# Memory projections as full-precision products of raw weights, a new division of the first convolution, and first-attention values with the value matrix stationary

## The chip, the cores and the metric

One Trainium2 chip; the kernel runs on one of its cores, as one launch. The time is the device time in microseconds (us) of that core. The kernel before takes 1420.38 us, the median of three runs (1419.74 to 1420.71). A core has five engines with a queue of instructions each: PE (TensorE, matrix products), DVE (VectorE), ACT (ScalarE), POOL (GpSimd) and SP (SyncE, which here only issues DMAs). Each executes its own queue in order; between engines only semaphores order the work.

## The reference, cut to what matters

Two transformer layers on 512 tokens of width 1024, all in float32. The change lies in the first:

```python
h = rmsnorm(x, norm_mix_g); proj = h @ w_in
q, k, v, qi, ki, wi, glu = split(proj)            # 8 query heads of 64, one key and value head
score = sum_h wi_h * relu(qi_h . ki)              # 4 index heads; keep the best 128 keys of a row
p = softmax(q . k / 8 over the chosen keys)       # 8 heads, 4 blocks of 128 queries
a_out = p @ v
u = causal_dwconv(ga * sigmoid(gg), conv_b_w, conv_b_b)   # 31 taps, 512 channels
b_out = silu(layernorm(u))                        # over the 512 channels
x = x + concat(a_out, b_out) @ w_out
hq = rmsnorm(x, norm_cross_g); m = rmsnorm(mem, norm_mem_g)   # mem: 256 rows of 1024
kc = m @ w_k_cross; vc = m @ w_v_cross            # the memory projections, two 1024 x 1024 weights
# then cross attention of hq on kc and vc, a feed-forward block, and the second layer
```

## The kernel before

Features lie on the 128 partitions and tokens on the free axis. Each weight matrix is streamed from HBM in chunks of 512 or 704 KB through two slots (`weights_raw`, slot = chunk number modulo 2). A chunk is split in two: ACT rounds it (`weights_high`, `high`, L661), POOL subtracts (`weights_low`, `low`, L584), and PE forms three products in the fast single-pass type for each block: high by high, high by low, low by high (`chunk`, L1615). The raw slot is free for the next DMA as soon as POOL has subtracted (`weight_low`).

The first layer up to the first part of its output projection is a plan written by hand, `FIRST_PLAN`: a list of items which every engine walks through in the same order, issuing its own part of each. After the 16 tiles of `w_in` come 35 steps. Step s holds, in this order: the logits of attention item s (PE L1820; an item is a head and a block of queries, 32 of them, in widths of 128, 256, 384 and 512 keys for 8 items each); on DVE the mask and row minimum (L1237); on ACT the exponential (L789); one to two "fills" taken from the list by `FILLS_AT`; the transposes of item s-2 (PE L1828, copied by ACT, L797); the values of item s-3 (PE L1839, p stationary, 64 columns of v moving); and taps of the convolution. A fill is half a chunk of a memory projection: 8 chunks for kc (256 columns, L1615), then 8 for vc (512 columns, L1725). ACT rounds chunk q+2 right behind chunk q (`fill_ends`).

The convolution has 4 blocks of 128 channels with 31 taps each. Two ways run side by side. `tap`: DVE multiplies and adds in one instruction (L1154), each waiting for the one before. `product`: ACT multiplies (L735) into one of two buffers, POOL adds (L633). ACT may start a product only when the addition two before it is done. Before, DVE has all taps of blocks 2 and 3 and the last 22 of block 1, in steps 0 to 24; ACT and POOL have block 0 and 9 taps of block 1, 40 products, 10 of which stand ahead of the steps and 30 in steps 0 to 23.

When all taps are there, step 25 has the mean of the layer norm (PE L1851, ones by conv), step 26 the variance (L1857), step 28 the spread of its factor over the partitions (`spread`, L1659) with four SiLU and four roundings on ACT (L814, L816), step 29 the low parts. From step 31 on, pieces of the output projection ("second", L1753) stand between the items. `norm` (DVE L1248) divides the values of a block of queries by their sums, `heads` (PE L1702) turns them, and `heads_out` splits them.

## Time and profile before

| | |
|---|---|
| median of 3 runs | 1420.38 us |
| the profiled execution: its time, its span | 1419.84 us, 1418.0 us |
| PE busy | 1367.1 us (96%) |
| DVE, ACT, POOL busy | 780.3, 539.2, 606.4 us |
| mean granted clock of PE | 0.983 of full |
| span of the 35 steps up to the first "second" piece | 131.1 to 253.2 us |

Times in rows are us from the start of the span unless marked ns. A matmul's row shows its whole passage through the array, so back-to-back rows overlap: the cost of one is read from start to start, not from its length. A float32 product shows as two records (x2), a product in the fast type as one, a float32 transpose as one.

### The profile page before, as it was taken

Reading aid. Unit: us, or ns where it says so; the run is one execution under the profiler, and the core shown is the slowest. Engines: PE = TensorE matmul, PEld = TensorE weight load, DVE = VectorE, ACT = ScalarE, POOL = GpSimd, SP = SyncE. Lnnn points to the kernel's source line nnn. Section 1 sums busy time; section 2 is a strip of 40 time slices with the busy share of each in tenths; the row PEclk is TensorE's granted clock in tenths of the full one; section 3 lists DMA queues with packets and bytes.
Section 4 is the critical chain, followed back from the end, with each engine's and each line's share of the span. In section 5 each row is a group of like instructions: output and inputs, shape, how many; then the busy total and the mean of one; then the engine's idle time right before and its main releaser. Section 6 shows DMA issues by size and latency. Waiting matters only on the chain.

```text
span 1418.0 us, 18066 instructions
## 1 busy us (share of the span) xinstructions
PE 1367.1 (96%) x6240; PEld 1096.9 (77%) x6240; DVE 780.3 (55%) x1091; ACT 539.2 (38%) x843; POOL 606.4 (43%) x295
## 2 busy tenths in 40 slices
PE   7999898999999999999999999999999999999997
PEld 5687776887777888888888777666778888888885
DVE  6698995253446777777523588655453333332222
ACT  4454667253333232223223353534342322323321
POOL 3487981342134444444444433122244444444341
PEclk8999999999999999999999999999999999999998
DMA  6122320121122232223322222111123232223321
GB/s 220 45 90 82 112 75 31 60 89 60 60 74 90 92 101 92 101 95 114 102 87 91 89 75 74 45 45 45 45 89 100 92 100 92 103 94 103 101 91 71
DMA packets 31876, 121.20 MB, mean 85 GB/s; under 512 B 3536, under 2 KB 3664, under 8 KB 31568
## 3 DMA queue, kind: packets, MB, share of 16 engines
q1 hardware_dynamic: 31392, 119.55, 25.0%
q10 hardware_dynamic: 432, 0.96, 0.3%
q8 instruction: 33, 0.54, 0.2%
q14 instruction: 19, 0.16, 0.0%
HBM read 118.40 MB, written 2.10 MB: 85 GB/s over the span
## 4 chain that ended last, share of the span: by engine, by line
PE 74%; issue 13%; POOL 5%; DVE 4%; ACT 2%; DMA 1%; POOLq 0%; SPq 0%; DVEq 0%; ACTq 0%
PE acc L1615 60%; POOL weights_low L584 3%; PE acc L1753 3%; POOL conv L633 2%; PE aux L1985 1%; PE aux L2005 1%; PE acc L1725 1%; PE aux L1987 1%; DVE aux L1154 1%; PE aux L1839 1%; PE aux L1820 1%; DVE a_low L1310 1%; DMA weights_raw<-w 1%; PE aux L1809 1%; PE aux L1995 1%
## 5 line engine op out<-in xcount | busy, mean ns | idle before, releaser
L584 POOL TENSOR_TENSOR weights_low<-weights_raw,weights_high 128x1024 fp32r<-128x1024 f32 (+1 forms) x204 | 524.6, 2572 | 781.9 <-ACT weights_high L661 778.9
L661 ACT CAST weights_high<-weights_raw 128x1024 fp32r<-128x1024 f32 (+1 forms) x202 | 221.8, 1098 | 511.3 <-PE acc L1615 478.8
L1615 PE MATMUL acc<-a_high,weights_high 128*128 128x512 f32 x976 | 390.0, 400 | 4.5 <-POOL weights_low L584 3.1
L1615 PE MATMUL acc<-a_high,weights_low 128*128 128x512 f32 x976 | 381.2, 391 | 0.0
L1615 PE MATMUL acc<-a_low,weights_high 128*128 128x512 f32 x976 | 380.8, 390 | 0.0
L1615 PEld LDWEIGHTS acc<-a_high,weights_high 128*128 128x128 f32 x976 | 183.9, 188 | 47.0 <-issue 6.3
L1615 PEld LDWEIGHTS acc<-a_low,weights_high 128*128 128x128 f32 x976 | 184.0, 189 | 39.5 <-issue 2.6
L1615 PEld LDWEIGHTS acc<-a_high,weights_low 128*128 128x128 f32 x976 | 183.8, 188 | 38.9
L1127 DVE TENSOR_TENSOR residual<-acc,residual 128x512 f32<-128x512 f32 (+1 forms) x64 | 44.0, 687 | 197.4 <-PE acc L1615 140.0
L1615 PE MATMUL acc<-h_high,weights_high 128*128 128x512 f32 x352 | 137.6, 391 | 0.0
L1615 PE MATMUL acc<-h_high,weights_low 128*128 128x512 f32 x352 | 137.0, 389 | 0.0
L1615 PE MATMUL acc<-h_low,weights_high 128*128 128x512 f32 x352 | 136.9, 389 | 0.0
L1392 DVE TENSOR_TENSOR h_low<-work,h_high 128x512 f32 x44 | 88.8, 2018 | 39.5 <-ACT h_high L892 39.5
L1386 DVE TENSOR_TENSOR work<-acc,row_factor 128x512 f32<-128x512 f32 x44 | 30.4, 692 | 105.5 <-PE acc L1615 105.5
L1615 PEld LDWEIGHTS acc<-h_high,weights_low 128*128 128x128 f32 x352 | 66.1, 188 | 13.8
L1615 PEld LDWEIGHTS acc<-h_high,weights_high 128*128 128x128 f32 x352 | 66.1, 188 | 13.5
L1615 PEld LDWEIGHTS acc<-h_low,weights_high 128*128 128x128 f32 x352 | 66.1, 188 | 13.4
L889 ACT ACTIVATE work<-work 128x512 f32<-128x512 f32 x44 | 27.8, 631 | 97.6 <-DVE work L1383 94.0
L1306 DVE TENSOR_TENSOR square_sum<-square_sum,square 128x512 f32<-128x512 f32 x20 | 51.5, 2576 | 20.2 <-ACT square L1040 9.9
L1154 DVE SCALAR_TENSOR_TENSOR aux<-glu,par,aux 128x512 f32<-128x512 f32 x78 | 58.8, 754 | 2.0
L1479 DVE TENSOR_TENSOR_SCAN left<-stay 128x128 f32<-128x128 f32 (+3 forms) x32 | 33.6, 1049 | 44.6 <-ACT stay L961 41.3
L1381 DVE SCALAR_TENSOR_TENSOR work<-gated,par,work 128x512 f32<-128x512 f32 x22 | 55.4, 2518 | 3.4 <-DVE work L1379 3.4
(347 smaller groups left out, 1920.2 us busy)
## 6 DMA issues: line engine op xcount, KB each, us to landing
weights_raw<-w SPq DMA_DIRECT2D x172, 512.0 KB, 3.2
weights_raw<-w SPq DMA_DIRECT2D x32, 704.0 KB, 4.0
residual<-xT SPq DMA_DIRECT2D x8, 256.0 KB, 7.2
out<-y_tok SPq DMA_DIRECT2D x4, 512.0 KB, 3.7
mem_raw<-memT SPq DMA_DIRECT2D x1, 1024.0 KB, 5.4
mem_tok<-mem SPq DMA_DIRECT2D x1, 1024.0 KB, 7.4
lru_weights<-blockdiag ACTq DMA_DIRECT2D x1, 512.0 KB, 3.4
sine<-positions ACTq DMA_DIRECT2D x1, 256.0 KB, 7.0
```

Source lines behind the costliest of these rows:

```text
L584: g.tensor_tensor(weights_low[:, s, 0:cols], weights_raw[:, s, 0:cols], weights_high[:, s, 0:cols].bitcast(F32), ALU.subtract).then_inc(we ...
L633: g.tensor_tensor(conv[:, b], conv[:, b], product[:, j % 2], ALU.add).then_inc(last_conv_steps, 1)
L661: a.copy(weights_high[:, s, 0:cols], weights_raw[:, s, 0:cols]).then_inc(weight_high, 1)
L1127: v.tensor_tensor(residual[:, bass.ds(n, 1)].rearrange("p a n -> p (a n)"), acc[:, s], residual[:, bass.ds(n, 1)].rearrange("p a n -> p (a ...
L1154: ins = v.scalar_tensor_tensor(dst, src, weight, sofar, ALU.mult, ALU.add)
L1306: v.tensor_tensor(total_ if to is None else to, total_, squares, ALU.add).then_inc(summed, 1)
L1381: own.then(v.scalar_tensor_tensor(work[:, 0], gated[:, 1:1 + T], dcol("fconv_w", c + 1), work[:, 0], ALU.mult, ALU.add))
L1386: v.tensor_tensor(work[:, 1], acc[:, 1], row_factor[:], ALU.mult).then_inc(tile_out[1], 1)
L1392: v.tensor_tensor(at(dst_low, i), work[:, 1], at(dst_high, i).bitcast(F32), ALU.subtract).then_inc(operand_low, 1)
L1479: own.then(v.tensor_tensor_scan(left[:, 0:w][:, ::-1], back, back, 1.0, ALU.mult, ALU.min))
L1615: last = t_.matmul(acc[:, bank, 0:cols], w[:, s, wide], x_[:, k0 + k, 0:cols], start=start and k == opens and n == 0, stop=stop and k == c ...
L1753: last = t_.matmul(acc[:, t], w[:, q % 2, wide], x_[:, block0 + k], start=k == 0 and n == 0, stop=k == 3 and n == 2)
```

## The change

- kc and vc are now float32 products straight from the raw chunk and from the scaled memory `m_raw`: one instruction for each block in place of three (L1731, L1742 of the new kernel). No rounding, no subtraction, no `m_high` and `m_low`. The gain of the memory norm is multiplied in by ACT, not POOL. A raw slot is now free only when PE has finished its chunk (`chunk_done`), for the 16 chunks of kc and vc and for the first two of the next matrix.
- The convolution: ACT and POOL take blocks 0 and 1 whole (62 products, 10 ahead of the steps and 52 in steps 0 to 21), DVE blocks 2 and 3 (62 taps in steps 0 to 20). Mean, variance, spread and low parts move from steps 25, 26, 28, 29 to 23, 24, 26, 27.
- Values: v is stationary, in two copies padded with zeros (`v_pad`), p moves with 128 columns, and the result comes out with features on partitions. The inverse sums are turned instead of the values: reciprocal (`total`) at step 8, 16, 24, 32, widened by ACT, turned by PE and copied by ACT one step later, multiplied in by DVE (`norm`) two steps later.
- `spread` turns the factor with a transpose in place of a float32 product, at all nine places where it is called.

```diff
-        m_high = sb("m_high", [P, KB, MB * P], F32R, s1)
-        m_low = sb("m_low", [P, KB, MB * P], F32R, s1)
+        m_raw = sb("m_raw", [P, KB, MB * P], where=s1)
...
-        v_tok = sb("v_tok", [P, QB, HALF], where=s1)
+        v_pad = sb("v_pad", [P, 2, QB, P], where=s1)
...
-        SHARED_TAPS = 9
-        PRODUCTS = [(1, k) for k in range(SHARED_TAPS)] + [(0, k) for k in range(TAPS)]
-        CONV = [(n, k) for n in (2, 3) for k in range(TAPS)] + [(1, k) for k in range(SHARED_TAPS, TAPS)]
+        PRODUCTS = [(n, k) for n in range(2) for k in range(TAPS)]
+        CONV = [(n, k) for n in (2, 3) for k in range(TAPS)]
...
-        BETWEEN = {5: [("key_turn", 1), ("glu_scale", 1), ("mem_high", 0, 4), ("mem_low", 0, 2), ("best",),
+        BETWEEN = {5: [("key_turn", 1), ("glu_scale", 1), ("best",),
                        ("key", 1), ("v",), ("mem_root",)],
...
-        CONV_STEPS, PRODUCT_STEPS = 25, 24
+        CONV_STEPS, PRODUCT_STEPS = 21, 22
...
+            if step >= 8 and step % A_HEADS == 0:
+                FIRST_PLAN.append(("total", step // A_HEADS - 1))
+            if step >= 9 and step % A_HEADS == 1:
+                FIRST_PLAN.append(("heads", step // A_HEADS - 1))
             if step >= 10 and step % A_HEADS == 2:
                 FIRST_PLAN.append(("norm", step // A_HEADS - 1))
             if step >= 11 and step % A_HEADS == 3 and step < len(DSA):
-                FIRST_PLAN += [("heads", step // A_HEADS - 1), ("heads_out", step // A_HEADS - 1)]
-            if step == 25:
+                FIRST_PLAN.append(("heads_out", step // A_HEADS - 1))
+            if step == 23:
                 FIRST_PLAN.append(("mean",))
+            if step == 24:
+                FIRST_PLAN.append(("variance",))
             if step == 26:
-                FIRST_PLAN.append(("variance",))
-            if step == 28:
                 FIRST_PLAN.append(("ln_spread",))
-            if step == 29:
+            if step == 27:
                 FIRST_PLAN.append(("ln_low",))
             if step >= 31:
                 FIRST_PLAN += SECOND[:1]
                 SECOND = SECOND[1:]
-        FIRST_PLAN += SECOND[:2] + [("heads", 3), ("heads_out", 3)] + SECOND[2:]
+        FIRST_PLAN += SECOND[:2] + [("heads_out", 3)] + SECOND[2:]
...
+        def splits(q):
+
+            return 1 + 2 * KB * (q == CHUNK["out"])
...
+            for first, end, used in ((2, CHUNK["kc"] // 2 + 1, weight_low),
+                                     (CHUNK["kc"] // 2 + 1, CHUNK["out"] // 2 + 1, chunk_done),
+                                     (CHUNK["out"] // 2 + 1, CHUNK["down"] // 2, weight_low)):
+                with sp.Fori(first, end) as m:
+                    for s in range(2):
+                        load(m, s, w8_chunk(2 * m + s), KB * P, used)
...
-                low((q + 2) // 2, q % 2, KB * P)
+                if not CHUNK["kc"] <= q + 2 < CHUNK["out"]:
+                    low((q + 2) // 2, q % 2, KB * P, splits(q + 2))
...
+            def high_after(q):
+
+                if not CHUNK["kc"] <= q + 2 < CHUNK["out"]:
+                    high(q // 2 + 1, q % 2, count=splits(q + 2))
...
-                elif what == "mem_high":
+                elif what == "mem_scale":
+                    act.wait_ge(memT_in, 16)
                     for k in range(*n):
-                        act.wait_ge(mem_scaled, k + 1)
-                        a.copy(m_high[:, k], mem_raw[:, k]).then_inc(mem_high, 1)
+                        a.activation(m_raw[:, k], m_raw[:, k], ACT.Copy, scale=col("g_mem", k)
+                                     ).then_inc(mem_scaled, 1)
                 elif what == "mem_root":
...
+                elif what == "total":
+                    act.wait_ge(inverse_ready, j + 1)
+                    if j:
+                        act.wait_ge(inverse_spread, j)
+                    a.copy(wide_inverse[:].rearrange("p (h d) -> p h d", d=HALF),
+                           head_inverse.rearrange("p (h d) -> p h d", d=1).broadcast_to([P, A_HEADS, HALF])
+                           ).then_inc(inverse_wide, 1)
+                elif what == "heads":
+                    act.wait_ge(inverse_spread, j + 1)
+                    if j:
+                        act.wait_ge(att_scaled, j)
+                    a.copy(att_inverse[:], turn_bank(what, j)[:]).then_inc(inverse_out, 1)
                 elif what == "heads_out":
-                    act.wait_ge(att_turned, j + 1)
...
+                elif what == "total":
+                    dve.wait_ge(prob_raw, A_HEADS * (j + 1))
+                    if j:
+                        dve.wait_ge(inverse_wide, j)
+                    v.reciprocal(head_inverse, head_total[j % 2]).then_inc(inverse_ready, 1)
                 elif what == "norm":
                     dve.wait_ge(heads_done, A_HEADS * (j + 1))
+                    dve.wait_ge(inverse_out, j + 1)
                     if j:
-                        dve.wait_ge(att_turned, j)
-                    own.then(v.reciprocal(head_inverse, head_total[j % 2]))
-                    v.tensor_tensor(att_tok[:].rearrange("p (h d) -> p h d", d=HALF),
-                                    aux[4][:].rearrange("p (h d) -> p h d", d=HALF),
-                                    head_inverse.rearrange("p (h d) -> p h d", d=1
-                                                           ).broadcast_to([P, A_HEADS, HALF]),
-                                    ALU.mult).then_inc(att_scaled, 1)
...
-                    last = t_.matmul(bank[:, tt * P:(tt + 1) * P],
-                                     factor[:, tt:tt + 1].broadcast_to([P, P]), ident[:],
-                                     start=True, stop=True)
+                    last = t_.transpose(bank[:, tt * P:(tt + 1) * P],
+                                        factor[:, tt:tt + 1].broadcast_to([P, P]), ident[:])
...
-                    pe.wait_ge(mem_low, KB)
+                    pe.wait_ge(mem_scaled, KB)
+                pe.wait_ge(chunk_landed[q % 2], 16 * (q // 2 + 1))
                 if n < KB:
                     if k == 0:
                         free(n % 2, TILE["kc"] // 2 + n // 2)
-                    chunk(q // 2, q % 2, end, q % 2, M, cols=MB * P, first=k)
+                    for i in range(k, end):
+                        last = t_.matmul(acc[:, n % 2, 0:MB * P], weights_raw[:, q % 2, i * P:(i + 1) * P],
+                                         m_raw[:, i], start=i == 0, stop=i == KB - 1)
+                    if end == KB:
+                        last.then_inc(chunk_done, 1)
                     return
                 part = n % 4
                 if part == 0 and k == 0:
                     for b in range(MB):
                         free(b, TILE["vc"] // 2 + (n - KB) // 4)
-                pe.wait_ge(weight_low, q + 1)
                 i = k // 4
                 for b in range(MB):
-                    rows, wide = slice(b * P, (b + 1) * P), slice(i * T, (i + 1) * T)
-                    for p_, (w, x_) in enumerate(((weights_high, m_high), (weights_high, m_low),
-                                                  (weights_low, m_high))):
-                        last = t_.matmul(acc[:, b], x_[:, 2 * part + i, rows], w[:, q % 2, wide],
-                                         start=part == 0 and i == 0 and p_ == 0,
-                                         stop=part == 3 and i == 1 and p_ == 2)
+                    last = t_.matmul(acc[:, b], m_raw[:, 2 * part + i, b * P:(b + 1) * P],
+                                     weights_raw[:, q % 2, i * T:(i + 1) * T], start=part == 0 and i == 0,
+                                     stop=part == 3 and i == 1)
                 if i:
                     last.then_inc(chunk_done, 1)
...
                 if at >= 2:
                     kind, j = BANKS[at - 2]
                     if kind == "heads":
-                        pe.wait_ge(operand_low, OP["a"] + j + 1)
+                        pe.wait_ge(inverse_out, j + 1)
                     else:
                         pe.wait_ge(probT_ready, j + 1)
...
-                        last = t_.matmul(aux[4][:, h * HALF:(h + 1) * HALF],
+                        last = t_.matmul(aux[4][:, h // 2 * P:(h // 2 + 1) * P], v_pad[:, h % 2, b],
                                          probT[:, j % 2, b * P:(b + 1) * P],
-                                         v_tok[:, b], start=b == 0, stop=b == qb)
+                                         start=h % 2 == 0 and b == 0, stop=h % 2 == 1 and b == qb)
                     last.then_inc(heads_done, 1)
                 elif what == "heads":
-                    pe.wait_ge(att_scaled, j + 1)
+                    pe.wait_ge(inverse_wide, j + 1)
                     bank_free(what, j)
-                    blocks_of(att_tok, turn_bank(what, j)).then_inc(att_turned, 1)
+                    blocks_of(wide_inverse, turn_bank(what, j)).then_inc(inverse_spread, 1)
                 elif what == "mean":
                     pe.wait_ge(conv_steps, len(CONV))
...
```

ACT around step 26, with what each instruction waits for: a cast is `high` of a chunk of the output projection, `probT` the copy of turned probabilities, `conv<-conv` the SiLU. Before:

```order
L789 ACTIVATE prob,small<-masked,small 128x512 [waits probT_done,logits_masked]
L797 COPY probT<-aux 128x512 [waits heads_done,probT_done]
L814 ACT_TABLE_LOAD
L814 ACTIVATE conv<-conv,par 128x512 [waits ln_scaled]
L816 CAST a_high<-conv 128x512 [waits act_steps]
```

Now:

```order
L817 COPY att_inverse<-aux 128x512 [waits att_scaled,inverse_spread]
L797 ACTIVATE prob,small<-masked,small 128x512 [waits probT_done,logits_masked]
L663 CAST weights_high<-weights_raw 128x1024 [waits chunk_done,chunk_landed0]
L805 COPY probT<-aux 128x512 [waits heads_done,probT_done]
L833 ACT_TABLE_LOAD
L833 ACTIVATE conv<-conv,par 128x512 [waits ln_scaled]
L835 CAST a_high<-conv 128x512 [waits act_steps]
```

The layer norm has come forward to the step in which the first chunk of the output projection is rounded; that cast now stands just ahead of a copy of probabilities and of the SiLU, and the chunk that it rounds is loaded only after PE has finished the last but one chunk of vc.

POOL inside the steps: `conv` is an addition of the convolution, `weights_low` a subtraction of a chunk. Before:

```order
L633 TENSOR_TENSOR conv<-conv,product 128x512 [waits last_conv_steps,products]
L584 TENSOR_TENSOR weights_low<-weights_raw,weights_high 128x1024 [waits weight_high]
L633 TENSOR_TENSOR conv<-conv,product 128x512 [waits last_conv_steps,products] x2
L584 TENSOR_TENSOR weights_low<-weights_raw,weights_high 128x1024 [waits weight_high]
L633 TENSOR_TENSOR conv<-conv,product 128x512 [waits last_conv_steps,products]
```

Now:

```order
L635 TENSOR_TENSOR conv<-conv,product 128x512 [waits last_conv_steps,products] x2
L596 TENSOR_TENSOR weights_low<-weights_raw,weights_high 128x1024 [waits weight_high]
L629 TENSOR_TENSOR glu<-glu,gate 128x512 [waits glu_gate]
L635 TENSOR_TENSOR conv<-conv,product 128x512 [waits last_conv_steps,products] x56
L596 TENSOR_TENSOR weights_low<-weights_raw,weights_high 128x1024 [waits weight_high] x6
```

The subtractions between the additions are gone, and the additions stand in one chain of 56, of which the last 51 belong to the steps.

## Rows read from the trace of the kernel before

**Rows 1.** Stretch: length, busy us of PE, PEld, DVE, ACT, POOL; clock, DMA.

```profile
135.30:218.40 83.10, 71.96 (x428) 60.64 (x428) 76.58 (x149) 55.45 (x121) 71.38 (x44) 0.94 0.27 89
218.40:253.20 34.80, 30.59 (x153) 23.34 (x154) 13.74 (x30) 25.70 (x43) 4.69 (x2) 0.85 0.07 24
```

**Rows 2.** Chain that ended last: start, us, what; its last tap, mean, first "second".

```profile
217.63 0.76 DVE conv L1154
218.44 3.70 PE aux L1851 x8
...
253.21 1.51 PE acc L1753 x6
```

**Rows 3.** Timeline and group of DVE, taps of the convolution.

```profile
199.36 3.13 DVE L1154 SCALAR_TENSOR_TENSOR aux<-glu,par,aux 128x512 f32<-128x512 f32 x4
...
L1154 DVE SCALAR_TENSOR_TENSOR aux<-glu,par,aux 128x512 f32<-128x512 f32 x78 | 58.8, 754 | 2.0
```

**Rows 4.** Timeline and group of POOL, additions of the convolution.

```profile
162.02 4.18 POOL L633 TENSOR_TENSOR conv<-conv,product 128x512 f32<-128x512 f32 x3
...
L633 POOL TENSOR_TENSOR conv<-conv,product 128x512 f32<-128x512 f32 x38 | 49.4, 1300 | 4.9 <-ACT product L735 2.6
```

**Rows 5.** Timeline of ACT, start of the steps; groups of products and quarter-size casts.

```profile
135.66 0.40 ACT L789 ACTIVATE prob<-masked,small 128x128 f32<-128x128 f32 x1 [2.72 <-DVE small L1237]
...
L735 ACT ACTIVATE product<-glu,par 128x512 f32<-128x512 f32 x38 | 26.9, 721 | 6.5 <-POOL conv L633 6.5
...
L759 ACT CAST m_high<-mem_raw 128x256 fp32r<-128x256 f32 x8 | 2.6, 401 | 0.0
```

**Rows 6.** Timeline of PE: a float32 product of 512 columns, then fast-type ones.

```profile
221.97 1.02 PE L1820 MATMUL aux<-kT,qT 128*128 128x512 f32 x2
...
223.06 0.39 PE L1725 MATMUL acc<-weights_high,m_low 128*128 128x512 f32 x1
223.29 0.40 PE L1725 MATMUL acc<-weights_low,m_high 128*128 128x512 f32 x1
```

**Rows 7.** Timeline of PE: half a chunk of kc, first and last of 12.

```profile
128.28 0.28 PE L1615 MATMUL acc<-m_high,weights_high 128*128 128x256 f32 x1
...
129.59 0.28 PE L1615 MATMUL acc<-m_high,weights_low 128*128 128x256 f32 x1
```

**Rows 8.** Timeline of PE: end of a fill, then values held up.

```profile
235.31 0.39 PE L1725 MATMUL acc<-weights_low,m_high 128*128 128x512 f32 x1
...
246.97 0.90 PE L1839 MATMUL aux<-v_tok,probT 128*128 128x64 f32 x3 [4.17 <-ACT probT L797]
```

**Rows 9.** Timeline of ACT: layer norm, exponential, cast, copies.

```profile
236.77 1.28 ACT L814 ACT_TABLE_LOAD   x1
238.75 0.81 ACT L814 ACTIVATE conv<-conv,par 128x512 f32<-128x512 f32 x1 [0.69 <-DVE conv L1272]
...
246.35 0.56 ACT L797 COPY probT<-aux 128x512 f32<-128x512 f32 x1
...
247.53 1.03 ACT L661 CAST weights_high<-weights_raw 128x1024 fp32r<-128x1024 f32 x1
248.47 1.26 ACT L721 ACTIVATE vc<-acc,small 128x512 f32<-128x512 f32 x2
249.62 0.59 ACT L797 COPY probT<-aux 128x512 f32<-128x512 f32 x1
```

**Rows 10.** DMA issues of the page: KB each, us to landing.

```profile
weights_raw<-w SPq DMA_DIRECT2D x172, 512.0 KB, 3.2
```

**Rows 11.** Chain: two spreads (801.00), and one set of four transposes (233.01).

```profile
801.00 1.92 PE aux L1659 x16
...
233.01 0.44 PE aux L1702 x4
```

**Rows 12.** Timelines of DVE and POOL: two SBUF inputs at once.

```profile
195.26 1.02 DVE L1154 SCALAR_TENSOR_TENSOR aux<-glu,par,conv 128x512 f32<-128x512 f32 x1
...
195.68 1.72 POOL L633 TENSOR_TENSOR conv<-conv,product 128x512 f32<-128x512 f32 x1
```

83 lines of the change are left out of this document (35 added, 48 removed).

## The prediction

> **What bounds the kernel now.** The page says that PE is busy throughout, which decides nothing for the steps of the first attention, the only stretch that the change rewrites: a busy PE there is one whose records overlap. So I went first to the busy time of each engine over two stretches. From the first mask at 135.3 us to the last tap, 83.1 us, DVE is busy for 76.6 us and POOL for 71.4, ACT for 55.5 [rows 1]. The chain of waits then says which of them ends last: it runs through the last tap (217.63, DVE) into the mean of the layer norm on PE at 218.44 [rows 2]. So 26 steps are paced by DVE, at some 3.2 us each, with POOL close behind. From the mean to the first piece of the output projection at 253.21 it is 34.8 us [rows 2], in which POOL is nearly idle and PE waits 4.17 us for a copy of probabilities at 246.97 [rows 8]: ACT is in the layer norm's SiLU from 238.75 and reaches that copy at 246.35 [rows 9]. Behind 253.2 PE is dense until the next stage.
>
> **The steps 0 to 22: from DVE to POOL.** DVE loses 22 of 84 taps. A run of four takes 3.13 us with the last one 0.75 long, so the pitch is 0.79, and 22 of them are 17.4 us [rows 3]. That is no gain by itself, since the same 22 taps go to ACT and POOL. ACT has room: 22 more products at 0.72 against 16 casts of 1.03 that go [rows 5, 9]. POOL loses 16 subtractions, but additions now follow one another in one chain of waits on itself. Three in a row take 4.18 us with a length of 1.30, so the pitch is 1.44; I use 1.43 [rows 4]. The steps hold 52 products, one of which opens block 1 and needs no addition: 51 x 1.43 = 72.9 us. They can't start before the first exponential (135.66 + 0.40 [rows 5]) and one product, so at 137.0, and they can't end before 209.9. POOL must also be fed. In a step ACT has an exponential, a copy and then the next product, about 2.0 us, and the two buffers cover two additions, 2.9 us less the product's own 0.72. That leaves about nothing, and three of every eight steps get one more ACT copy of some 0.6 us (widening, taking back and splitting the inverse sums). Six of these fall in the run, some 2 to 4 us. I take 4 us of idle POOL, between 0 and 8 (DVE, the pacing engine of before, is idle for 6.5 of 83.1 [rows 1]). The mean then starts at 214.0, against 218.44: **-4.4 us**.
>
> PE does not pace these steps, but it comes close. A float32 product of 512 columns starts at 221.97 and the fast-type product behind it ends its turn at 223.06, 0.23 being one turn, so it costs 0.86 [rows 6]; three fast products cost 3 x 0.23 = 0.70. At 256 columns three cost 0.36 (twelve records from 128.28 to 129.59, pitch 0.119 [rows 7]), and the float32 one, by half the columns, 0.43. Half a chunk thus goes from 1.4 to 1.72 us, +0.3 for each of 31 halves in the steps, 9.6 us more PE in all. Before the mean it lies beside POOL's chain: 26 halves at 1.72 and 22 steps of 0.6 to 1.6 us make some 68 us, under 72.9. Waits of PE for subtractions go. Values keep two records for each block, at 128 columns in place of 64. No row shows that form here; a fast product of 256 columns, as many column passes as a record of 128 in float32, takes its turn in 0.12 [rows 7], so 160 records can't cost over 19 us where they stand now at some 16; I give the difference nothing, as it lies under POOL's chain but for the last steps, and at most +1 us.
>
> **From the mean on.** The mean is now in step 23, with eight logits still to come instead of six. Two more steps of PE work are logits 2 x 0.86, turned probabilities and values of 384 keys, together 3.6 us, and one more half chunk, 1.7; three other halves are 0.3 longer. Sum 6.3 us. Then there are two new waits, both from ACT's order. A raw slot is now held until PE is done with its chunk. In step 26 PE ends chunk 14 of the 16, the DMA starts only then and needs 3.2 us [rows 10], and ACT, in order, waits for it with the cast, behind which stand the copy of probabilities and the whole layer norm, which has come forward to this same step. From the end of the fill: 3.3 to landing, 0.95 cast, 0.55 copy, 1.3 table load (before, it ran while ACT waited), and from the first SiLU to the end of the held-up copy 8.2 (238.75 to 246.91 [rows 9]): 14.3 us. Before, it was 11.4 (235.54 to 246.97 [rows 8]). That is +2.9. In step 30 the last chunk does the same: 3.3, then cast, two copies of vc and the copy of probabilities, 2.7 (247.53 to 250.21 [rows 9]), 6.0 in all, while PE has transposes, values, logits and transposes to do, 2.6. That is +3.4. Before, the slot was free as soon as POOL had subtracted, long ahead of the cast. Ends for the two waits: 0, if the cast's wait fell beside other work, and 7.5. Tail: 6.3 + 6.3 = **+12.6 us**.
>
> **The rest.** A spread is 0.96 us (two in 1.92), four transposes are 0.44 [rows 11]: -0.52 at each of nine calls. One is in the steps and counted with the tail's rounding; one stands at the start, where it pays for the four gain products (0.40 each [rows 5]) that ACT now has in front of the index heads' ReLU, so I set that part to 0, between -0.5 and +1.6. Seven later ones stand in dense PE work: **-3.6 us**, between -4 and -1.5. The second write of v, the two memsets and the wider wait for p cost nothing: they lie under DVE's wait for the key's turn and at the start under the first loads. Dropped m_high and m_low casts were never waited for.
>
> **Sum**, against the profiled execution: -4.4 + 12.6 - 3.6 = +4.6, so 1419.84 + 4.6 = 1424.4 us. The median of the runs before lies 0.54 above that execution, so 1425.0.
>
> **A page against the trace.** The only tap with both inputs in SBUF took 1.02 us where the others take 0.75, and the addition beside it 1.72 in place of 1.30 [rows 3, 4, 12]. The Trainium skill ("SBUF — State Buffer", section "Who interferes with whom") says that a DVE instruction with two SBUF inputs contends with a GpSimd instruction that reads SBUF; by that rule the new low part of the attention result, now read from `att` instead of PSUM, would meet POOL's additions, and the trace agrees as far as that one pair goes. It would add some 0.4 us to the chain in each of the two places that fall into it, under 1 us to the sum, which I leave out; the change also removes the pair itself.
>
> **Rivals.**
> - *The landings hide.* If ACT's two waits for the raw chunk cost PE nothing (the DMA is short and PE has something to do), the sum is 4.6 - 6.3 = -1.7: 1418.7, no change that shows. For it: PE has other items queued. Against it: the copies that PE needs stand behind the cast on ACT, and rows 8 and 9 show PE idle behind just such a queue. 15%.
> - *The steps really get shorter (faster).* DVE was the pace; if additions back to back run at their own length, 1.30, and POOL is fed with 2 us of idling, the last one ends at 137.0 + 66.3 + 2 = 205.3, and the sum is -13.1 + 12.6 - 3.6 = -4.1: 1416.3. It decides from a pitch under 1.35. For it: DVE and ACT have slack. Against it: every run of additions in the trace shows 0.1 us between them. 22%.
> - *PE starves chunk by chunk.* With the raw slot held, each of 14 loads must fit in PE's time for one chunk, at least 3.44 us against 3.3. If queueing makes it 4 us where two halves stand close, that is 0.5 us for about 12 chunks, +6: 1431. 13%.
>
> The forecast has the other 50%.
>
> **How the numbers follow.** About 0.2%, 2.8 us, is what the measurement can tell from no change. The forecast's own range is 1418 to 1431, from the idling (-4 to +4) and the waits (-6.3 to +1.2). Some 6 of its 50 points fall within 0.2%. With the first rival and parts of the others this gives faster 0.24, within 0.2% 0.22, slower 0.54. The range is 1413.5 to 1431.5: it takes in the faster rival and its neighbours, and leaves out the far end of the starving one.
>
> **What would show it right or wrong.** Right: no SP wait on subtractions in the steps, POOL's additions back to back in a stretch of 73 to 81 us; mean at 210 to 218; ACT waiting some 3.4 us ahead of a cast of `weights_high` in steps 26 and 30; PE with two waits of over 2 us in step 28 and one in step 31; first "second" piece at 258 to 265 instead of 253.2; spreads of four records in 0.44. Wrong: POOL with long gaps or additions under 1.35 apart, no wait of ACT for a landing, PE waiting for chunks in the fills, or the tail from mean to "second" below 42 us.

## The result, and the profile after

The changed kernel takes 1433.85 us (median of four runs, 1431.16 to 1436.55), the kernel before 1420.06 beside it: ratio 1.0099, 95% interval 1.0085 to 1.0113. Slower, as forecast, but by 13.8 us and not by 5; the range ended at 1431.5. The profiled execution took 1431.16 us, its span 1429.4, against 1419.84 and 1418.0.

The span splits at four marks of PE: the first product of the index heads (the tiles before it are the same in both kernels), the first exponential, the mean, the first "second" piece. The first row is of the kernel before (timeline of PE), the second of the one after:

```profile
49.46 1.35 PE L1809 MATMUL aux<-kiT,qiT 128*128 128x256 f32 x5
```

```profile
46.16 1.02 PE L1826 MATMUL aux<-kiT,qiT 128*128 128x256 f32 x4
```

Ahead of any place where the change can cost, the execution of after is 3.3 us early. Of that, the transposed spread is 0.5; the spread itself already begins 2.8 us earlier. Other kernels of this study, the same up to there, reach this mark between 46.0 and 48.8 us: most of it is the execution, not the edit. So stretches are compared here, not instants. Busy time and clock in them, after the change (columns as in [rows 1]):

```profile
133.20:215.30 82.10, 72.68 (x325) 51.36 (x325) 59.51 (x122) 57.96 (x130) 65.47 (x51) 0.96 0.26 84
215.30:266.20 50.90, 38.78 (x169) 25.95 (x169) 14.39 (x33) 27.99 (x48) 4.70 (x2) 0.84 0.09 32
```

The steps up to the mean take 82.1 us (82.7 before, from the exponential at 135.7 to 218.4), although two attention steps have left them. From the mean to "second" it is 50.9 where it was 34.6. DVE has lost 17 us of work in the steps (76.2 to 59.5), as computed, and nobody is the faster for it. The whole difference of the spans, by stretch:

| stretch | before | after | difference | forecast |
|---|---|---|---|---|
| start to index | 49.5 | 46.2 | -3.3 | 0 |
| index to first exponential | 86.2 | 87.0 | +0.8 | 0 |
| steps, to the mean | 82.7 | 82.1 | -0.6 | -4.4 |
| tail, mean to "second" | 34.6 | 50.9 | +16.3 | +12.6 |
| "second" to the end | 1165.0 | 1163.2 | -1.8 | -3.6 |
| sum | 1418.0 | 1429.4 | +11.4 | +4.6 |

**Who paces the steps.** POOL's timeline after (start, length, what; in brackets the idle time before and who ended it), the answer to [rows 4]:

```profile
134.38 29.58 POOL L635 TENSOR_TENSOR conv<-conv,product 128x512 f32<-128x512 f32 x21 [4.38 <-ACT product L742]
...
164.86 1.26 POOL L635 TENSOR_TENSOR conv<-conv,product 128x512 f32<-128x512 f32 x1 [0.89 <-ACT product L742]
169.14 4.10 POOL L635 TENSOR_TENSOR conv<-conv,product 128x512 f32<-128x512 f32 x3 [3.02 <-ACT product L742]
175.11 2.96 POOL L635 TENSOR_TENSOR conv<-conv,product 128x512 f32<-128x512 f32 x2 [1.87 <-ACT product L742]
```

21 additions in 29.58 us: pitch 1.41, as forecast. Three further gaps (0.80, 1.22, 1.15) follow to 208.2; with the three shown POOL is idle for 8.95 us between additions, where I had taken 4. The first gaps begin at one place, here in the timelines of ACT and of PE:

```profile
159.83 0.72 ACT L742 ACTIVATE product<-glu,par 128x512 f32<-128x512 f32 x1 [0.69 <-POOL conv L635]
161.23 0.72 ACT L742 ACTIVATE product<-glu,par 128x512 f32<-128x512 f32 x1 [0.69 <-POOL conv L635]
161.86 0.60 ACT L810 COPY wide_inverse<-small 128x512 f32<-128x512 f32 x1
```

```profile
162.52 1.11 PE L1718 MATMUL aux<-ident,wide_inverse 128*128 128x128 f32 x4 [3.61 <-ACT wide_inverse L810]
163.43 1.06 PE L1837 MATMUL aux<-kT,qT 128*128 128x256 f32 x2
164.28 3.54 PE L1731 MATMUL acc<-m_raw,weights_raw 128*128 128x256 f32 x8
```

```profile
168.07 0.37 ACT L805 COPY probT<-aux 128x256 f32<-128x256 f32 x1 [2.32 <-PE aux L1845]
```

The widened inverse (new) stands on ACT behind three products, and each product waits for POOL to give back one of two buffers. PE, in order, waits 3.61 us for it, and the logits of the next step are queued behind; DVE waits 3.69 us for them before its mask at 164.52. Behind the wait half a chunk of kc (eight records) takes 3.54 us, where the eleven such halves before it in the steps take 1.89. The turned probabilities stand behind that half on PE, their copy on ACT waits 2.32 us for them, the next products stand behind the copy, and so POOL has nothing to add from 166.12 to 169.14. The windows of 163.4 to 168.0 and of 247.2 to 256.2, behind another long wait, show why the half took so long; the third is one of dense work for comparison:

```profile
163.40:168.00 4.60, 4.60 (x15) 3.59 (x14) 0.43 (x2) 2.12 (x5) 1.83 (x2) 0.54 0.00 0
247.20:256.20 9.00, 7.99 (x24) 5.64 (x25) 4.32 (x9) 3.01 (x8) 0.00 (x0) 0.50 0.00 0
256.40:260.00 3.60, 3.60 (x19) 2.36 (x18) 0.70 (x2) 0.81 (x2) 0.00 (x0) 1.00 0.14 26
```

The granted clock is 0.54 and 0.50, the lower of its two levels (1.2 GHz against 2.4), after waits of 3.61 and 5.30 us: PE pays for such a wait twice.

**Who holds up the tail.** ACT, then DVE, then PE after the change, the answer to [rows 8, 9]:

```profile
236.22 1.04 ACT L663 CAST weights_high<-weights_raw 128x1024 fp32r<-128x1024 f32 x1 [3.73 <-DMA weights_raw<-w]
237.17 0.58 ACT L805 COPY probT<-aux 128x512 f32<-128x512 f32 x1
237.76 1.28 ACT L833 ACT_TABLE_LOAD   x1
...
246.66 0.56 ACT L805 COPY probT<-aux 128x512 f32<-128x512 f32 x1
247.12 0.62 ACT L820 CAST a_high<-att 128x512 fp32r<-128x512 f32 x1
...
261.71 1.04 ACT L663 CAST weights_high<-weights_raw 128x1024 fp32r<-128x1024 f32 x1 [3.57 <-DMA weights_raw<-w]
```

```profile
247.77 0.69 DVE L1275 TENSOR_TENSOR a_low<-att,a_high 128x512 fp32r<-128x512 f32 x1 [10.31 <-ACT a_high L820]
248.38 2.49 DVE L1294 TENSOR_TENSOR a_low<-conv,a_high 128x512 fp32r<-128x512 f32 x4
250.78 0.68 DVE L1255 CUSTOM_DVE_ANT_0 masked<-aux,score 128x512 f32<-128x512 f32 x1
```

```profile
237.80 1.16 PE L1856 MATMUL aux<-probT,v_pad 128*128 128x128 f32 x8 [2.34 <-ACT probT L805]
...
247.27 2.08 PE L1856 MATMUL aux<-probT,v_pad 128*128 128x128 f32 x8 [5.30 <-ACT probT L805]
...
256.39 1.88 PE L1742 MATMUL acc<-weights_raw,m_raw 128*128 128x512 f32 x4
...
264.45 2.07 PE L1856 MATMUL aux<-probT,v_pad 128*128 128x128 f32 x8 [3.55 <-ACT probT L805]
```

ACT waits for both landings (3.73 and 3.57), as the prediction had it, and PE for the copies behind them: 2.34 us right behind the first cast, 5.30 behind the layer norm that follows it, 3.55 behind the second cast. What the prediction did not have is the DVE fence: the mask at 250.78, whose logits PE had done by 239.8, stands on DVE behind a low part that waits 10.31 us for ACT, and then behind the four low parts of the layer norm, which used to stand two steps later.

The remaining counterparts came out as forecast: landing 3.3 us against 3.2 [rows 10], and a pair of spreads 0.96 against 1.92 [rows 11] (the page's DMA row, and the chain):

```profile
weights_raw<-w SPq DMA_DIRECT2D x172, 512.0 KB, 3.3
```

```profile
814.85 0.96 PE aux L1676 x8
```

### The profile page after: what moved, and what is told of

Read it like the earlier page. It is cut to its first block, busy times and chain, and to the rows that moved or that the text cites. A ratio compares the mean times of both kernels' runs of the same rounds, so it can differ in the third digit from the quotient of the medians.

```text
span 1429.4 us, 17820 instructions
## 1 busy us (share of the span) xinstructions
PE 1371.1 (96%) x6108; PEld 1084.8 (76%) x6108; DVE 764.1 (53%) x1072; ACT 543.7 (38%) x857; POOL 584.3 (41%) x285
## 4 chain that ended last, share of the span: by engine, by line
PE 73%; issue 12%; POOL 6%; DVE 4%; ACT 3%; DMA 1%; POOLq 0%; SPq 0%; DVEq 0%; ACTq 0%
PE acc L1632 60%; POOL conv L635 3%; PE acc L1770 3%; POOL weights_low L596 2%; PE aux L2002 1%; PE aux L2022 1%; DMA weights_raw<-w 1%; PE aux L2004 1%; PE aux L1856 1%; DVE a_low L1328 1%; PE aux L2012 0%; PE acc L1696 0%; PE aux L2038 0%; DVE residual L1148 0%; PE aux L1837 0%
## 5 line engine op out<-in xcount | busy, mean ns | idle before, releaser
L596 POOL TENSOR_TENSOR weights_low<-weights_raw,weights_high 128x1024 fp32r<-128x1024 f32 (+1 forms) x188 | 486.6, 2588 | 794.1 <-ACT weights_high L663 791.0
L663 ACT CAST weights_high<-weights_raw 128x1024 fp32r<-128x1024 f32 (+1 forms) x186 | 205.4, 1104 | 511.8 <-PE acc L1632 471.6
L635 POOL TENSOR_TENSOR conv<-conv,product 128x512 f32<-128x512 f32 x60 | 77.1, 1285 | 25.4 <-ACT product L742 18.7
L1632 PEld LDWEIGHTS acc<-h_high,weights_low 128*128 128x128 f32 x352 | 66.1, 188 | 13.8
L1497 DVE TENSOR_TENSOR_SCAN left<-stay 128x128 f32<-128x128 f32 (+3 forms) x32 | 33.6, 1049 | 44.0 <-ACT stay L980 40.7
```

Source lines behind the costliest of these rows:

```text
L596: g.tensor_tensor(weights_low[:, s, 0:cols], weights_raw[:, s, 0:cols], weights_high[:, s, 0:cols].bitcast(F32), ALU.subtract).then_inc(we ...
L635: g.tensor_tensor(conv[:, b], conv[:, b], product[:, j % 2], ALU.add).then_inc(last_conv_steps, 1)
L663: a.copy(weights_high[:, s, 0:cols], weights_raw[:, s, 0:cols]).then_inc(weight_high, count)
L1497: own.then(v.tensor_tensor_scan(left[:, 0:w][:, ::-1], back, back, 1.0, ALU.mult, ALU.min))
L1632: last = t_.matmul(acc[:, bank, 0:cols], w[:, s, wide], x_[:, k0 + k, 0:cols], start=start and k == opens and n == 0, stop=stop and k == c ...
```

## The experiments

The change has four separable parts: S (spreads by transposes), F (full-precision memory projections from the raw weights, so no casts and subtractions for their 16 chunks), D (division of the convolution, with mean and layer norm two steps earlier) and V (the values' matrix stationary, with the turned inverse). Each kernel below was timed beside the one before; a ratio is against it, of 1419 to 1420 us. "Steps" and "tail" are the stretches of the table above, in its profiled execution.

| run | median | ratio, 95% | steps | tail |
|---|---|---|---|---|
| s_spreads (S) | 1415.99 | 0.9972, 0.9962 to 0.9981 | 82.7 | 34.0 |
| fs_no_div_no_val (F, S) | 1411.63 | 0.9946, 0.9932 to 0.9959 | 77.5 | 34.6 |
| fds_no_values (F, D, S) | 1434.14 | 1.0088, 1.0068 to 1.0109 | 78.6 | 50.2 |
| fvs_old_division (F, V, S) | 1418.36 | 0.9988, 0.9978 to 0.9999 | 82.2 | 34.5 |
| a_late_mean | 1415.75 | 0.9984, 0.9970 to 0.9997 | 82.8 | 34.9 |
| a_ln_later | 1426.17 | 1.0044, 1.0029 to 1.0059 | 81.3 | 42.1 |
| fs_19_taps | 1411.56 | 0.9937, 0.9915 to 0.9959 | 74.8 | 34.9 |
| fvs_total_first | 1412.73 | 0.9949, 0.9932 to 0.9965 | 77.4 | 32.8 |
| a_total_first | 1429.76 | 1.0065, 1.0045 to 1.0086 | 77.5 | 51.1 |
| a_late_total_first | 1415.38 | 0.9964, 0.9951 to 0.9976 | 78.9 | 33.6 |
| a_ln_cast_later | 1425.11 | 1.0034, 1.0019 to 1.0048 | 82.5 | 42.2 |
| a_ring4 | 1425.04 | 1.0060, 1.0038 to 1.0081 | 76.3 | 49.1 |
| a_late_ring4 | 1411.44 | 0.9949, 0.9933 to 0.9964 | 77.0 | 33.3 |
| fds_late_ring4 | 1410.21 | 0.9937, 0.9922 to 0.9952 | 76.2 | 36.1 |
| a_cast_only | 1430.80 | 1.0069, 1.0047 to 1.0092 | 82.1 | 45.7 |
| a_ln_low_only | 1432.45 | 1.0084, 1.0061 to 1.0107 | 81.2 | 47.7 |

### Which part costs

**s_spreads.** The kernel before, and in `spread`:

```diff
-                    last = t_.matmul(bank[:, tt * P:(tt + 1) * P],
-                                     factor[:, tt:tt + 1].broadcast_to([P, P]), ident[:],
-                                     start=True, stop=True)
+                    last = t_.transpose(bank[:, tt * P:(tt + 1) * P],
+                                        factor[:, tt:tt + 1].broadcast_to([P, P]), ident[:])
```

> The kernel before with one edit: the spreads of per-token factors over the partitions are transposes (36 instructions) in place of matmuls against the identity (72 records of 0.44 to 0.48 us). Theory A (the prediction's step): each of the seven later spreads gets 0.52 us shorter on PE and the spreads stand on the path, so 1420.1 - 3.6 = 1416.5 us. Theory B (what the changed kernel's trace shows after its second projection starts): only 1.9 us come back, 1418.2 us. Rival: they lie beside other waits and nothing moves, 1420.1 us.

Measured 0.9972, that is -4.0 us (-2.7 to -5.4): theory A. Seven later spreads at 0.52 are 3.6 us; with as much from the first and from the layer norm's it would be 4.7, which the interval takes in too. (A record of the old spread is 0.27 us long in the trace, not 0.44 to 0.48.)

**fs_no_div_no_val.** S and all edits of F, of which the core is:

```diff
-                    chunk(q // 2, q % 2, end, q % 2, M, cols=MB * P, first=k)
+                    for i in range(k, end):
+                        last = t_.matmul(acc[:, n % 2, 0:MB * P], weights_raw[:, q % 2, i * P:(i + 1) * P],
+                                         m_raw[:, i], start=i == 0, stop=i == KB - 1)
```

> The kernel before with the transposes for spreads and the full-precision memory projections, but with the old division of the first convolution and the old form of the attention's values. Theory A (landing waits): exp 0 starts about 2 us earlier, the fp32 half chunks cost 1 us more on PE in the tail, and the casts of the two first chunks of the second projection wait for their landing, 2.9 to 3.7 us each, so +5 against the spreads alone: about 1422.5 us. Rival B (the landings hide behind the DVE pace): about 1416.5 us. Rival C (PE becomes the bound by its 0.3 us more per half chunk, 30 half chunks): over 1426 us.

Measured 1411.63: all three theories fall, on the fast side. Its windows, steps and tail, against [rows 1]:

```profile
133.30:210.80 77.50, 74.09 (x350) 52.73 (x350) 75.21 (x147) 42.10 (x107) 38.12 (x30) 1.00 0.27 90
210.80:245.40 34.60, 30.74 (x143) 21.33 (x143) 13.67 (x30) 25.79 (x43) 4.70 (x2) 0.85 0.16 52
```

The steps shrink by 5.2 us although DVE, which paced them, has nearly the same work (75.2 us against 76.2): it was idle for 6.5 us of 82.7 before and is for 2.3 now. Its listed waits of before, 2.8 us for PE and 1.3 for ACT, are gone. A likely reason is that PE no longer waits for POOL's subtractions (POOL busy 71.4 us before, 38.1 now) and has the full clock (1.00 against 0.94); no run parts the two. The largest wait of that kind in the kernel before, in the steps:

```profile
PE acc L1615 <- POOL weights_low L584: 3.9, 3, 1.9
```

And the landings cost the tail nothing (34.6, as before), as rival B had it. ACT's timeline of this run at the first of them:

```profile
215.29 2.42 ACT L806 ACTIVATE gate<-conv 128x512 f32<-128x512 f32 x4 [2.70 <-DVE conv L1263]
217.69 0.72 ACT L789 ACTIVATE prob<-masked,small 128x512 f32<-128x512 f32 x1
...
220.68 1.05 ACT L655 CAST weights_high<-weights_raw 128x1024 fp32r<-128x1024 f32 x1 [2.18 <-issue]
```

The squares and an exponential lie beside the landing, ACT waits 2.18 us instead of 3.73, and the layer norm's SiLU is still two steps away.

**fds_no_values** and **fvs_old_division** leave one part out of the changed kernel. Core of the first (values as before) and of the second (division as before, with mean, variance and layer norm at 25, 26, 28, 29):

```diff
-                        last = t_.matmul(aux[4][:, h // 2 * P:(h // 2 + 1) * P], v_pad[:, h % 2, b],
+                        last = t_.matmul(aux[4][:, h * HALF:(h + 1) * HALF],
                                          probT[:, j % 2, b * P:(b + 1) * P],
+                                         v_tok[:, b], start=b == 0, stop=b == qb)
```

```diff
-        PRODUCTS = [(n, k) for n in range(2) for k in range(TAPS)]
+        SHARED_TAPS = 9
+        PRODUCTS = [(1, k) for k in range(SHARED_TAPS)] + [(0, k) for k in range(TAPS)]
...
-        CONV_STEPS, PRODUCT_STEPS = 21, 22
+        CONV_STEPS, PRODUCT_STEPS = 25, 24
```

> The changed kernel without the edit of the attention's values: the old values (probabilities stationary), the division by the row sums on VectorE and the turn of the result on PE. Theory A (the knots around the turned inverse cost POOL its idle time in the steps, and the tail loses most of the rest): the mean starts at about 212 us in place of 215.3, the tail stays near 50, so about 1429 to 1430 us. Rival D (the values' edit costs nothing anywhere, the division and the tail are all): as the changed kernel, 1433.9 us. Rival V (the values' edit is the main loss): under 1424 us.

> The changed kernel with the old division of the first convolution (nine taps of column block 1 on POOL, the rest on VectorE) and the layer norm at its old steps. Theory A (the tail is what costs, since the mean now comes two steps earlier than the steps can be finished): steps paced by VectorE again, mean near 217, tail 34.8 plus the landing waits of two casts (6) and 1 for PE, so about 1423 to 1425 us. Rival D (division is neutral, the loss sits in the full-precision projections and the values): 1431 us or more. Rival E (division was the whole loss): 1416.5 us.

Without V the time stays at 1434.14: by the stretches theory A (steps 3.5 us shorter, tail 50.2), by the median rival D, since that execution is 5.6 us longer behind "second" (see the last section). Without D it is 1418.36, 15.5 us less than the changed kernel and nearest to rival E; its tail of 34.5 has nothing of the 6 us of landing waits that theory A put there. So D is the loss: 22.5 us on top of F and S, 15.5 on top of F, V and S. V costs 6.7 us where DVE paces the steps.

### Why the tail costs 16 us

**a_late_mean.** The new division, with the work spread over as many steps as before:

```diff
-        CONV_STEPS, PRODUCT_STEPS = 21, 22
+        CONV_STEPS, PRODUCT_STEPS = 25, 24
...
-            if step == 23:
+            if step == 25:
                 FIRST_PLAN.append(("mean",))
```

(and variance, scaling and low parts at 26, 28 and 29.)

> The changed kernel with its own division (all of column blocks 0 and 1 on POOL), but its adds and taps spread over the steps up to 23 and 24, the mean at step 25 and the layer norm at its steps of before. Theory A (the placement: the steps' time is set by POOL's 51 adds and the knots and does not depend on how many attention steps stand in it, so each step moved out of it is bought back in the tail at its full price): steps 82 us as now, tail 34.6 in place of 51.2, 1433.9 - 16.6 = about 1417 us. Rival B (the two steps' PE work lengthens the steps): about 1421 to 1424 us. Rival C (the tail is long because of the landing waits of the casts and not of the placement): over 1430 us.

Measured 1415.75, theory A. Its windows:

```profile
134.80:217.60 82.80, 77.24 (x354) 54.46 (x355) 60.17 (x127) 60.28 (x137) 65.62 (x51) 0.98 0.25 83
217.60:252.50 34.90, 30.71 (x141) 21.33 (x139) 13.04 (x27) 24.58 (x41) 4.70 (x2) 0.85 0.14 46
```

The same 51 additions, two more attention steps beside them, and 82.8 us in place of 82.1: the two steps cost 0.7 us here, and with the layer norm's place 16.0 us behind the mean.

**a_ln_later** moves only the layer norm's scaling and low parts back (`step == 26` to 28, `step == 27` to 29); **a_ln_low_only** only the low parts; **a_cast_only** only the casts of the second projection's first two chunks, in `fill_ends`:

```diff
-                high_after(q)
+                if n >= 14:
+                    held.append([q, 2])
+                else:
+                    high_after(q)
```

where `held` is emptied behind the second probT copy that follows; **a_ln_cast_later** does the first and the third together.

> The changed kernel with the mean and variance where it has them (steps 23 and 24), but the layer norm's scaling at step 28 and its low parts at step 29, as before the change, in place of 26 and 27. Theory A (in the trace of the changed kernel VectorE's masked logits of step 28 stand behind a low part that waited 10.3 us for ScalarE and four low parts of the layer norm): 4 to 6 us come back, about 1429 us. Rival (ScalarE's eight layer-norm operations and two table loads only move to a later step and hold up that one): 1433 to 1434 us.

> The run a_ln_later with the casts of chunks 0 and 1 of the second projection one step later on ScalarE, behind the copy of the next turned probabilities. Theory (the prediction's landing waits): the one wait of 3.6 us for the landing that is left there goes, 1426.2 - 3.6 = 1422.6 us. Rival (TensorE's next half chunk and logits only move into the gap, and the next wait ends last): 1425 to 1426 us. What then still separates it from a_late_mean's 1415.7 us is the placement of the mean itself.

> The changed kernel with nothing moved but the casts of chunks 0 and 1 of the second projection, each one step later on ScalarE. Prediction's own step (two landing waits, +2.9 and +3.4 us, are new in the tail): 6.3 us come back, about 1427.5 us. Rival (a_ln_cast_later gave 1 us at most where the layer norm stood later; what ends last is the copy behind the layer norm's eight operations, wherever the cast stands): 1431 to 1433 us. Between them, if the wait in step 26 holds up the layer norm that has come forward and the one in step 30 lies in slack: 1430 us.

> The changed kernel with nothing moved but the four low parts of the layer norm on VectorE, from step 27 back to step 29, their step before the change; its scaling stays at step 26. Theory (the chain of the changed kernel holds 2.49 us of these four ahead of the mask of step 28): 2.5 us less, about 1431.3 us. Rival (the mask of step 28 waits for ScalarE all the same, since the low part of the attention in front of it waits 10.3 us for ScalarE's layer norm): 1433.9 us, and the whole 7.7 us of a_ln_later came from ScalarE's order.

Tails, from the windows of a_ln_later, a_cast_only and a_ln_low_only, and PE in a_cast_only at its last half chunk of vc:

```profile
215.90:258.00 42.10, 35.23 (x168) 23.57 (x169) 14.59 (x32) 27.18 (x46) 4.71 (x2) 0.92 0.11 39
```

```profile
217.00:262.70 45.70, 37.27 (x169) 25.08 (x169) 15.98 (x32) 26.22 (x45) 2.34 (x1) 0.85 0.08 28
```

```profile
214.50:262.20 47.70, 36.65 (x168) 24.78 (x169) 14.48 (x33) 27.84 (x48) 4.70 (x2) 0.89 0.10 34
```

```profile
256.90 2.48 PE L1751 MATMUL acc<-weights_raw,m_raw 128*128 128x512 f32 x4
```

The casts alone give back 5.2 us of the tail (4.3 by the ratios, between the rival and the prediction's step), the low parts alone 3.2 (2.1), the layer norm's place 8.8 (7.8), and the casts nothing more once the layer norm has moved (42.2, the rival of a_ln_cast_later). The last half chunk of vc parts the casts' 5.2 us: from there to "second" it is 9.8 us in the changed kernel (256.39 to 266.2) and 5.8 in a_cast_only (256.90 to 262.7). So 4.0 belong to the landing in step 30 and 1.2 to the one in step 26, the other way round than the expectation's 1430 us had it, though its number came near.

So the tail's 16.3 us are 8.8 of order (two landings and four low parts ahead of a mask) and 7.2 to 7.5 of the two steps and the half chunk, the difference between 42.1 and 34.6 to 34.9. Of these 7.5, only 4.5 are busy time of PE (35.2 us against 30.7 in fs_no_div_no_val, the mean clocks being 0.92 and 0.85); the other 3 are more waiting. The layer norm's move does more than the expectation had: DVE's low part waits 4.07 us for ACT there in place of 10.31, and one landing falls beside other work. The intervals of a_ln_low_only and of the changed kernel overlap, so its 2 to 3 us rest on the trace.

### Why the steps stay at 82 us

**fvs_total_first** and **a_total_first.** One item of the plan moves up, ahead of the step's taps and products:

```diff
+            if step >= 8 and step % A_HEADS == 0:
+                FIRST_PLAN.append(("total", step // A_HEADS - 1))
             if step < CONV_STEPS:
...
-            if step >= 8 and step % A_HEADS == 0:
-                FIRST_PLAN.append(("total", step // A_HEADS - 1))
```

> The run fvs_old_division with one move: the reciprocal of the row sums (VectorE) and its widening (ScalarE) stand ahead of the taps and products of their step in place of behind them. Theory (the values' edit costs its 6.7 us because TensorE waits 4.2 us for the widened inverse in two places and VectorE behind it): about 4 us less, 1414.4 us. Rival (the cost is TensorE's own: it is busy 107.2 us from the first exponential to the second projection, against 104.8 without the edit, and the waits lie in slack): 1418.4 us.

> The changed kernel with the reciprocal of the row sums and its widening ahead of the taps and products of their step, nothing else moved. Theory (knots: the widened inverse stands behind three POOL-paced products on ScalarE and TensorE waits for it at the start of the next step, 3.6 us at step 9): the stretch from the first exponential to the mean, 82 us, comes down by the same 5 us as in fvs_total_first if the wait is what held POOL idle (8.6 us): 1428.5 us. Rival (POOL's 51 adds of 1.415 us, 72.2 us, and their waits for products set the stretch whatever stands beside them): 1 us or nothing, 1433 us.

Both theories hold: -5.5 us by the ratios (0.9988 to 0.9949), most of V's 6.7, and -4.8 (1.0099 to 1.0065), steps 82.2 to 77.4 and 82.1 to 77.5. In the changed kernel the rows of waits "for whom, times, longest" were and are:

```profile
PE aux L1718 <- ACT wide_inverse L810: 4.8, 2, 3.6
```

```profile
POOL conv L635 <- ACT product L742: 8.5, 6, 4.4
DVE masked L1255 <- PE aux L1837: 3.4, 2, 2.8
PEld aux L1718 <- ACT wide_inverse L810: 0.2, 1, 0.2
```

The first is of the changed kernel, the others of a_total_first, where 4.4 of POOL's 8.5 us are the start at the first product. So POOL's gaps are 4.1 us there in place of 8.95.

**a_ring4.** The changed kernel with four product buffers:

```diff
-                    if adds_before(i - 1):
-                        act.wait_ge(last_conv_steps, adds_before(i - 1))
-                    ins = a.activation(product[:, i % 2], src, ACT.Copy, scale=weight)
+                    if i > 3 and adds_before(i - 3):
+                        act.wait_ge(last_conv_steps, adds_before(i - 3))
+                    ins = a.activation(product[:, i % 4], src, ACT.Copy, scale=weight)
```

> The changed kernel with four product buffers between ScalarE and POOL in place of two, nothing moved. Theory (the steps are paced by the pair of ScalarE's products and POOL's adds, each waiting for the other: ScalarE waits 15.4 us for POOL in 29 places and POOL 13.3 us for ScalarE in 7): POOL's idle time goes, the stretch from the first exponential to the mean comes from 82 down to 76 or 77 us, the tail stays 51, 1428.5 us. Rival (two buffers are enough, the knots at the turned inverse alone hold the steps): 1433 us.

The steps come down to 76.3 us, as the theory had it, and the ratio by 5.5 us (the median, 1425.0, by 8.8). POOL's timeline there:

```profile
134.27 35.27 POOL L635 TENSOR_TENSOR conv<-conv,product 128x512 f32<-128x512 f32 x25 [4.39 <-ACT product L742]
171.41 2.95 POOL L635 TENSOR_TENSOR conv<-conv,product 128x512 f32<-128x512 f32 x2 [1.87 <-ACT product L742]
175.16 34.12 POOL L635 TENSOR_TENSOR conv<-conv,product 128x512 f32<-128x512 f32 x24 [0.80 <-ACT product L742]
```

2.7 us of gaps are left of 8.95. The chain of additions alone, 51 x 1.41 = 72, is then the bound, as forecast. It was through the ring of two buffers that the order of ACT's items reached the additions.

**fs_19_taps** takes ten taps from DVE where F and S stand alone (`SHARED_TAPS = 19`). **a_late_total_first**, **a_late_ring4** and **fds_late_ring4** add the repairs up: late mean and early inverse; with four buffers; with four buffers and without V.

> The run fs_no_div_no_val with nineteen taps of column block 1 on POOL in place of nine, mean and layer norm at the old steps. VectorE has ten taps of 0.754 us less (7.5 us) of the 75.3 it is busy in the steps; TensorE is busy 74.1 of 77.6 us there. Theory PE (TensorE becomes the bound at once): 3 us less, about 1408.5 us. Rival DVE (the whole 7.5 comes off): 1404 us. Rival POOL (49 adds of 1.4 us and their waits for ScalarE's products pace the steps): 1411 us or more.

> The run a_late_mean with the same move of the reciprocal and the widening. Theory (both repairs add up, since one shortens the steps and the other fills them): 1415.7 - 5 = about 1411 us, level with fs_no_div_no_val, so that the changed division and the values' edit are worth nothing either way once they are placed well. Rival (the steps are bound by TensorE, busy 76.5 of 81.7 us, as soon as the waits go): 1413 to 1414 us.

> The run a_late_total_first with four product buffers. Theory (POOL's 9.8 us of waits go and TensorE, 76.5 us of work in a stretch of 78.9, becomes the bound): the stretch comes down to about 77 us, 1413 us. Rival (nothing left to gain, the stretch is TensorE's already): 1415.4 us.

> Full-precision projections, transposed spreads and the new division, but the old form of the attention's values; adds and taps spread over the steps to 23 and 24, mean at step 25, four product buffers. Theory (the values' edit is worth nothing or costs TensorE 2 us): about 1410 to 1411 us, a little below a_late_ring4 and level with fs_no_div_no_val. Rival (the values' edit helps once its waits are gone): above a_late_ring4.

fs_19_taps, by its windows:

```profile
134.70:209.50 74.80, 73.49 (x351) 52.73 (x351) 69.23 (x137) 48.67 (x117) 49.94 (x39) 1.00 0.28 93
```

PE is busy for 73.5 of 74.8 us: it is the bound there, and 2.7 us of the 7.5 taken from DVE came off, as theory PE had it; the median (1411.56, run to run 1406.1 to 1413.0) can't show them. a_late_total_first gained 3.9 us in the steps and 1.3 in the tail, but 2.8 by the ratio and nothing in the median, 1415.38 where the theory had 1411 and the rival 1413 to 1414: neither is borne out. a_late_ring4 came down to the 77 us of its theory and fds_late_ring4 to its 1410 us. These two stand at 1411.44 and 1410.21, apart by less than their intervals: no worth of V shows where little waits for it. With the late mean, the early inverse and four buffers the changed kernel is 22 us faster than it is. fds_late_ring4 is 9 us faster than the kernel before and has the lowest median of the study, but fs_no_div_no_val, with nothing of D and V, is level with it within the intervals: S and F are the gain, and what D and V can add to it is not measurable.

## Why the prediction was wrong, step by step

- **Steps 0 to 22, -4.4: wrong in size, -0.6.** The pacing engine, the count and the pitch of the additions were right (51 at 1.41 to 1.43). The failed number is "I take 4 us of idle POOL": it was 8.95, outside the 0 to 8 given, and the additions themselves took 1.1 us less than 51 x 1.43. I had added up ACT's own work for the inverse (0.6 us each) and not asked who waits for its result. With that one item moved (a_total_first) the gaps are 4.1 us and the steps 4.6 shorter; with four buffers (a_ring4) 2.7 and 5.8.
- **"Two more steps of PE work ... Sum 6.3": near by some luck,** 7.2 to 7.5 by a_ln_later against a_late_mean and fs_no_div_no_val, of which only 4.5 are PE's work and the rest waiting, which the term did not have.
- **Two new waits for landings, +6.3: right in mechanism, 5.2** by a_cast_only (4.3 by the ratios, give or take 3). ACT waited 3.73 and 3.57 us where 3.4 was named. But the first cost 1.2 and not 2.9, the second 4.0 and not 3.4, and with the layer norm two steps later moving both casts gave back nothing that shows.
- **Left out: the layer norm's low parts on DVE, +3.2.** The prediction followed ACT's and PE's queues past the moved items and not DVE's. Listing what the moved `ln_low` stands in front of, the mask of step 28, would have shown it.
- **Early part 0 and later spreads -3.6:** +0.8, inside the range given, and, by s_spreads, -4.0 for all spreads. The 0.8 come with F (86.2 us in s_spreads, 87.1 in fs_no_div_no_val); that they are ACT's gain products is not shown. In the execution profiled only -1.8 shows behind "second"; at 266.2 to 331.0 its clock is 0.97 where before had 1.00.
- **fp32 on PE hidden under POOL: right.** PE was busy for 72.7 of 82.1 us, and it came to bound the steps only where everything else was taken out (fs_19_taps).
- **The rivals.** "Landings hide" is what happens in a_late_mean and fs_no_div_no_val, where the layer norm comes later (in the second, squares and an exponential lie beside the landing), but not in the changed kernel. "Steps really get shorter" failed on POOL's pitch. "PE starves chunk by chunk" did not occur: the steps have no row of PE waiting for a landing.

The missing 8.9 us of the median (1433.85 against 1425.0) are, in the terms above, 3.8 of the steps, 3.7 of the tail and 0.8 of the early part, 8.3 in all. What is left, 0.6, is below what runs of one kernel differ by. The profiled execution alone shows less, 6.8: its start was 3.3 us early, and behind "second" it has 1.8 us less gain than forecast.

The rule of the Trainium skill that was weighed ("SBUF — State Buffer", section "Who interferes with whom") is borne out by the trace, at the price named, under 1 us. The trace of the changed kernel has 60 additions of the convolution on POOL; all take 1.26 to 1.31 us but two, and these two lie beside the two low parts out of SBUF in the steps (205.22 here, and 176.19, beside an addition of 1.54):

```profile
205.22 0.69 DVE L1275 TENSOR_TENSOR a_low<-att,a_high 128x512 fp32r<-128x512 f32 x1 [2.88 <-ACT a_high L820]
```

```profile
205.42 1.63 POOL L635 TENSOR_TENSOR conv<-conv,product 128x512 f32<-128x512 f32 x1
```

That is 0.6 us on the chain for both, and the removed pair (1.72) had cost 0.4. In the kernel before, with that operand in PSUM, the additions beside the same low parts took 1.27 to 1.29. In a_ring4 it was once the low part that was held up, 1.65 us at 198.00 beside an addition begun at 197.83.

A step of the plan was thus valued wrongly in the change itself: the steps' stretch had a length of its own, set by the additions, and two attention steps stood in it for nothing. Ending the additions "earlier" by two steps ended them at the same time and left 16 us of work and waits exposed.

## What to carry to other kernels

Moving a milestone to an earlier step of a plan gains nothing if the stretch before it is paced by an engine whose work stays the same: check in microseconds, not in steps, and keep as much other work beside the pacing chain as it can cover. For each item moved or added, look on every engine at what is queued behind it; here the three costs that were missed or mis-sized (products ahead of a copy that PE needs, a cast ahead of a copy, four subtractions ahead of a mask) were all of that kind, and most of each went away by moving one item within its step or by one or two steps. A ring of two buffers between in-order engines passes the pace of the slower to everything behind the faster one; here two more buffers were worth as much as the move.
